# The feed-forward stage of a decoder layer as seven block products in place of eight

## What is computed

```python
D_MODEL = 1024
D_FF = 2816
    x = x + merged @ wo
    h = rmsnorm(x, g_ffn)
    a, u = jnp.split(h @ w_gu, 2, axis=-1)
    return x + (jax.nn.silu(a) * u) @ w_dn
```

## Time and profile before

| what | value |
|---|---|
| time, median of 3 runs | 996.94 us (992.06 to 997.19) |
| time of the profiled execution | 996.81 us |
| its span | 995.0 us |
| busy over the span: PE, DVE, ACT, POOL | 97%, 51%, 34%, 8% |
| the feed-forward stage | about 583 to 981 us of the span |

### The profile page before, as it was taken

The page is one execution under the profiler, slowest core; times in us unless marked ns, Lnnn a source line. Parts: engine busy times, 40 slices in busy tenths (PEclk is TensorE's granted clock), DMA queues, the critical chain, the costliest instruction groups (busy, mean ns, idle before and its releaser), DMA issues.

```text
span 995.0 us, 18231 instructions
## 1 busy us (share of the span) xinstructions
PE 967.9 (97%) x7611; PEld 945.0 (95%) x7611; DVE 507.7 (51%) x933; ACT 335.9 (34%) x559; POOL 77.6 (8%) x107
## 2 busy tenths in 40 slices
PE   6999999999999899999999999999999999999997
PEld 5899999999989889899999999999999999999997
DVE  5735556544887472635355565554445555333232
ACT  7344223444544350422222342222222222222222
POOL 0100013011210200111023000000000000000000
PEclk9899999999999999999999999999999999999999
DMA  7582326432320766122222345222222222222302
GB/s 240 153 262 42 48 77 95 156 108 77 98 65 1 218 192 200 43 86 85 86 86 85 127 147 189 85 88 92 99 96 95 86 85 75 85 75 80 111 1 91
DMA packets 104909, 104.77 MB, mean 105 GB/s; under 512 B 11130, under 2 KB 101752, under 8 KB 104492
## 3 DMA queue, kind: packets, MB, share of 16 engines
q1 hardware_dynamic: 101224, 92.51, 30.3%
q0 software_dynamic: 3552, 11.08, 3.7%
q10 hardware_dynamic: 52, 0.01, 0.0%
HBM read 97.74 MB, written 15.45 MB: 114 GB/s over the span
## 4 chain that ended last, share of the span: by engine, by line
PE 86%; SPq 3%; DVE 3%; ACT 2%; issue 2%; DMA 1%; POOL 1%; ACTq 0%; DVEq 0%; POOLq 0%
PE acc L466 74%; SPq L698 3%; PE acc L1168 1%; PE acc L1081 1%; POOL mt L854 1%; PE acc L1057 1%; PE acc L935 1%; PE acc L924 1%; PE acc L895 1%; PE acc L1041 1%; PE acc L1252 1%; ACT h_hi L1562 1%; DVE w_lo L449 0%; PE acc L1069 0%; DVE mt L1670 0%
## 5 line engine op out<-in xcount | busy, mean ns | idle before, releaser
L466 PE MATMUL acc<-h_hi,w_hi 128*128 128x256 f32 (+1 forms) x1520 | 462.0, 304 | 3.1 <-DVE w_lo L449 2.1
L466 PE MATMUL acc<-h_lo,w_hi 128*128 128x256 f32 (+1 forms) x1520 | 439.2, 289 | 0.0
L466 PE MATMUL acc<-h_hi,w_lo 128*128 128x256 f32 (+1 forms) x1504 | 433.0, 288 | 0.0
L466 PEld LDWEIGHTS acc<-h_hi,w_hi 128*128 128x128 f32 x1520 | 287.6, 189 | 12.0 <-issue 5.1
L466 PEld LDWEIGHTS acc<-h_lo,w_hi 128*128 128x128 f32 x1520 | 288.0, 189 | 4.1 <-issue 2.4
L439 ACT ACTIVATE w_hi<-raw 128x1024 fp32r<-128x1024 f32 (+1 forms) x135 | 140.9, 1043 | 444.9 <-PE acc L466 444.9
L466 PEld LDWEIGHTS acc<-h_hi,w_lo 128*128 128x128 f32 x1504 | 285.0, 189 | 0.0
L449 DVE TENSOR_TENSOR w_lo<-raw,w_hi 128x1024 fp32r<-128x1024 f32 (+1 forms) x134 | 164.0, 1224 | 107.6 <-ACT w_hi L439 102.9
L466 PE MATMUL acc<-s_hi,w_hi 128*128 128x256 f32 (+1 forms) x352 | 101.6, 288 | 0.0
L466 PE MATMUL acc<-s_lo,w_hi 128*128 128x256 f32 (+1 forms) x352 | 101.3, 288 | 0.0
L466 PE MATMUL acc<-s_hi,w_lo 128*128 128x256 f32 (+1 forms) x352 | 100.7, 286 | 0.0
(11 more groups left out here) (348 smaller groups left out, 1122.6 us busy)
## 6 DMA issues: line engine op xcount, KB each, us to landing
raw<-in_w_in SPq DMA_DIRECT2D x25, 1024.0 KB, 5.3
raw<-in_w_gate_up SPq DMA_DIRECT2D x22, 1024.0 KB, 4.9
raw<-in_w_down SPq DMA_DIRECT2D x8, 1024.0 KB, 4.7
rev<-tab POOLq DMA_DIRECT2D x1, 4352.0 KB, 19.4
ring<-in_cache_dsa_kv SPq DMA_DIRECT2D x4, 1024.0 KB, 7.3
raw<-in_w_out SPq DMA_DIRECT2D x4, 1024.0 KB, 5.1
out<-in_cache_dsa_kv SPq DMA_DIRECT2D x2, 2016.0 KB
ring<-in_cache_moba_k SPq DMA_DIRECT2D x48, 64.0 KB, 2.1
```

What stands on the lines that cost most here:

```text
L466: ins = nc.tensor.matmul(acc[:, bank, 0:HALF[half]], a[:, k, :], two(b[:, kx + k, :], half), start=first and k == k0 and c == 0, stop=last ...
```

## The change

Outputs, inputs and tokens of each product are cut in two: a pair of output tiles `m`, a pair of input tiles `k` (even and odd), two halves of 272 tokens. The 2x2 by 2x2 block product is then formed with seven products (a form of Strassen's, with chained sums) for eight. `gate` and `up` are 11 pairs of output tiles each with 4 pairs of input tiles (`depth` 4); `down` is 4 pairs of output tiles, its 11 pairs of input tiles in four chunks of 2, 3, 3 and 3 (`KPS`). That makes 38 pairs, with 7 products each: a stream of 266 products, each of 3 x depth matmuls of 272 columns.

- Four sums of weight blocks for each pair go to GpSimd (`w_sums`), each over depth x 128 columns; one is written in place over `raw`.
- High and low parts of the seven weight operands are made product by product, 128 x (depth x 128), in a ring of six slots, five products ahead (`w_highs` on ACT, `w_lows` on DVE).
- Seven activation operands for each pair of input tiles: DVE forms four sums of 272 columns (`b_sum`), ACT the high parts, DVE the low parts, for `h` during the output projection and for `s` after each `up`.
- Products share partial sums through PSUM: ACT copies a bank into the bank that the next product adds to (`bank_seeds`), or into SBUF (`u2p5`), four copies a pair. DVE takes four results of 272 columns a pair, and scales or adds the first half of the tokens in one further instruction (`second_half`).
- The multiplication of the gate by its sigmoid moves from DVE to GpSimd (`gated_up`). `h_hi`, `h_lo`, `s_hi`, `s_lo` give way to buffers of seven operands.
- The virtual times, banks and semaphores follow; the last norm and the stores stay as they were but for their banks.

The diff, cut to its core:

```diff
+        h7_hi = Map(h_at)("h7_hi", [P, KD // 2, 7, TH], F32R)
+        ga = Map(h_at + 4 * (KD // 2) * 7 * TH)("ga", [P, 2, T])
         m = Map(region)
-        s_hi, s_lo = (m(n, [P, KF, T], F32R) for n in ("s_hi", "s_lo"))
-        sg = m("sg", [P, 2, T])
-        gx = sq
+        s7_hi = m("s7_hi", [P, 3, 7, TH], F32R)
+        h7_lo = m("h7_lo", [P, KD // 2, 7, TH], F32R)
+        wsum = m("wsum", [P, 2, 2, 512])
+        wx_hi, wx_lo = (m(n, [P, 2, 512], F32R) for n in ("wx_hi", "wx_lo"))
+        sv = m("sv", [P, 8, TH])
+        xs2 = m("xs2", [P, 2, TH])
+        s7_lo = m("s7_lo", [P, 3, 7, TH], F32R)
+        u2p5 = m("u2p5", [P, 2, TH])
...
-        for j in range(0, KF, 2):
-            add_load([(0, 0, rows(w_gu, 0, KD, j * P, 256))], KD)
-            add_load([(0, 0, rows(w_gu, 0, KD, D_FF + j * P, 256))], KD)
-        n_gu = len(blocks)
-        DOWN = ((0, 8), (8, 16), (16, 22))
-        for j in range(0, KD, 2):
-            for k0, k1 in DOWN:
-                add_load([(0, 0, rows(w_dn, k0, k1, j * P, 256))], k1 - k0)
...
+        KPS = (2, 3, 3, 3)
+        FIRST = (0, 2, 5, 8)
+        pairs = []
+        for c in range(len(KPS)):
+            for m_ in range(KPS[c]):
+                pairs.append(("gate", c, FIRST[c] + m_))
+                if m_ == 0 and c > 0:
+                    pairs += [("down", c - 1, j) for j in range(KD // 2)]
+                pairs.append(("up", c, FIRST[c] + m_))
+        pairs += [("down", len(KPS) - 1, j) for j in range(KD // 2)]
+        NPAIR = len(pairs)
...
+        stream = []
+        for n in range(NPAIR):
+            if follows(n):
+                if n:
+                    stream += [(n - 1, 4), (n - 1, 3)]
+                stream += [(n, p) for p in (1, 5, 6, 2, 7)]
+            else:
+                stream += [(n, 1), (n - 1, 4), (n - 1, 3)] + [(n, p) for p in (6, 5, 7, 2)]
+        stream += [(NPAIR - 1, 4), (NPAIR - 1, 3)]
+        pos = {np_: i for i, np_ in enumerate(stream)}
+        RING, LEAD = 6, 5
+        B_SLOT = {1: 0, 3: 1, 2: 2, 5: 3, 6: 4, 7: 5, 4: 6}
...
+        def w_source(n, p):
+            if p in (1, 2, 4, 7):
+                return w_part(n, *{1: (0, 0), 2: (0, 1), 4: (1, 1), 7: (1, 0)}[p])
+            return w_sum(n, 0 if p == 5 else 1)
...
+            if n - 3 >= ffn_load:
+                sp.wait_ge(w_lo_done, n_wout + pos[n - 3 - ffn_load, 3] + 1)
...
+                def w_sums():
+                    for n in range(NPAIR):
+                        at = pos[n, 1]
+                        yield tm(at - 5)
+                        pool.wait_ge(mm_done, mm_at[n_merge])
+                        w_ready(pool, n)
+                        if n >= 2:
+                            pool.wait_ge(w_lo_done, n_wout + pos[n - 2, 3] + 1)
+                        done = sem("w_sum")
+                        nc.gpsimd.tensor_tensor(w_sum(n, 0), w_part(n, 1, 0), w_part(n, 1, 1), ALU.add).then_inc(done, 1)
+                        yield tm(at - 4)
+                        pool.wait_ge(done, 4 * n + 1)
+                        nc.gpsimd.tensor_tensor(w_sum(n, 1), w_sum(n, 0), w_part(n, 0, 0), ALU.subtract).then_inc(done, 1)
+                        yield tm(at - 2.5)
+                        nc.gpsimd.tensor_tensor(w_part(n, 1, 0), w_part(n, 0, 0), w_part(n, 1, 0), ALU.subtract).then_inc(done, 1)
+                        yield tm(at - 1)
+                        pool.wait_ge(done, 4 * n + 3)
+                        pool.wait_ge(w_lo_done, n_wout + pos[n, 6] + 1)
+                        nc.gpsimd.tensor_tensor(w_sum(n, 1), w_part(n, 0, 1), w_sum(n, 1), ALU.subtract).then_inc(done, 1)
+                def gated_up():
+                    g = 0
+                    for n in range(NPAIR):
+                        kind, c, j = pairs[n]
+                        if kind == "gate":
+                            yield lag(n, T_GATE)
+                            for m in range(2):
+                                pool.wait_ge(sem("sg_done"), 2 * j + m + 1)
+                                nc.gpsimd.tensor_tensor(ga[:, m, :], ga[:, m, :], sg[:, m, :], ALU.mult).then_inc(sem("t_done"), 1)
+                Side(w_sums(), gated_up()).until(Side.END / 2)
...
+                def claim(n):
+                    for name in ("b", "c"):
+                        nc.tensor.matmul(bank(n, name), h7_hi[:, 0, 0, 0:P], h7_hi[:, 0, 0, :], start=True, stop=True)
+                def product(i):
+                    n, p = stream[i]
+                    kind, c, j = pairs[n]
+                    hi, lo, slot = w_slot(i, False), w_slot(i, True), B_SLOT[p]
+                    b_his, b_los, q0 = (s7_hi, s7_lo, 4 + FIRST[c]) if kind == "down" else (h7_hi, h7_lo, 0)
+                    name = {1: "a", 2: "a", 5: "e", 3: "e", 6: "b", 7: "c", 4: "c"}[p]
+                    pe.wait_ge(w_lo_done, n_wout + i + 1)
+                    if p == 1 and n >= 2:
+                        pe.wait_ge(ffn_ev, evacs[n - 2, 2])
+                    if p == 5 and n >= 2:
+                        pe.wait_ge(ffn_ev, evacs[n - 2, 3])
+                    if p in (6, 7):
+                        pe.wait_ge(seeded, seeds[n, "b" if p == 6 else "c"])
+                    if p == 4:
+                        pe.wait_ge(ffn_ev, evacs[n, 7])
+                    if p == 3:
+                        pe.wait_ge(seeded, seeds[n, "p5"])
+                    for k in range(depth(n)):
+                        if n == 0 or (kind == "down" and j == 0):
+                            pe.wait_ge(b_lo, 2 * KD + b_ready(q0 + k, slot))
+                        for z, (a, b) in enumerate(((hi, b_his), (hi, b_los), (lo, b_his))):
+                            ins = nc.tensor.matmul(bank(n, name), a[:, k, :], b[:, k, slot, :], start=p in (1, 5) and k == 0 and z == 0,
+                                                   stop=k == depth(n) - 1 and z == 2, skip_group_check=True)
+                    ins.then_inc(mm_done, 1)
...
-                        nc.scalar.activation(h_hi[:, k, :], xT[:, k, :], ACT.Copy, scale=vecs[:, 8 + k:9 + k]).then_inc(sem("h2_hi_done"), 1)
+                        if k >= 2 and k % 2 == 0:
+                            act.wait_ge(b_lo, 2 * KD + k // 2)
+                        nc.scalar.activation(s_tile[:, k % 2, :], xT[:, k, :], ACT.Copy, scale=vecs[:, 8 + k:9 + k]).then_inc(sem("hs_done"), 1)
...
+                def b_his(q, slots, hi):
+                    nc.scalar.copy(hi[:, slots, :], sv[:, 1 + slots.start:1 + slots.stop, :]).then_inc(b_hi, 1)
...
+                def w_highs():
+                    for i in range(len(stream)):
+                        n, p = stream[i]
+                        yield tm(i - LEAD) + 0.005 if i >= 4 else n_wout - 0.94 + 0.05 * i
+                        w_ready(act, n)
+                        slot_free(act, i)
+                        if p in (5, 6, 7, 3):
+                            act.wait_ge(sem("w_sum"), 4 * n + {5: 1, 6: 2, 7: 3, 3: 4}[p])
+                        nc.scalar.activation(w_slot(i, False), w_source(n, p), ACT.Copy).then_inc(w_hi_done, 1)
...
+                def bank_seeds():
+                    for i, n, what in copies:
+                        yield tm(i + 1)
+                        act.wait_ge(mm_done, products_done + i + 1)
+                        if what == "b":
+                            src, dst = bank(n, "a"), bank(n, "b")
+                        elif what == "c":
+                            if n >= 2:
+                                act.wait_ge(ffn_ev, evacs[n - 2, 4])
+                            src, dst = bank(n, "b"), bank(n, "c")
+                        elif what == "u2":
+                            if n >= 1:
+                                act.wait_ge(ffn_ev, evacs[n - 1, 3])
+                            src, dst = bank(n, "b"), u2p5[:, 0, :]
+                        else:
+                            if n >= 1:
+                                act.wait_ge(ffn_ev, evacs[n - 1, 7])
+                            src, dst = bank(n, "e"), u2p5[:, 1, :]
+                        nc.scalar.copy(dst, src).then_inc(seeded, 1)
...
+                def b_sum(out, a, b, name):
+                    nc.vector.tensor_tensor(sv[:, out, :], sv[:, a, :], sv[:, b, :], ALU.subtract).then_inc(sem(name), 1)
+                def b_low(slots, hi, lo):
+                    nc.vector.tensor_tensor(lo[:, slots, :], sv[:, 1 + slots.start:1 + slots.stop, :], hi[:, slots, :].bitcast(F32),
+                                            ALU.subtract).then_inc(b_lo, 1)
...
+                        b_sum(4, 0, 1, "b_sum")
+                        b_sum(6, 2, 0, "b_sum")
+                        dve.wait_ge(sem("b_sum"), 4 * q + 1)
+                        b_sum(5, 2, 4, "b_sum")
+                        dve.wait_ge(sem("b_sum"), 4 * q + 3)
+                        b_sum(7, 3, 5, "b_sum")
+                        yield n_merge + 2 * q + 2.7
+                        dve.wait_ge(b_hi, 2 * KD + q + 1)
```

(103 more changed lines are left out.)

285 lines of the change are left out of this document (176 added, 109 removed).

## The result

The changed kernel takes 1072.32 us (median of 4 runs, 1072.08 to 1076.13) against 994.81 us before (4 runs): a ratio of 1.079, 95% interval 1.075 to 1.083. Its profiled execution has a span of 1070.3 us. The side was forecast, the size was not: 77.5 us more, where 21.7 were predicted.

A forecast was written before the change was run, and what follows sets the result against it. PE bounds the old kernel; in the changed stage, POOL additions and DVE two-input instructions taking turns would. 996.8 + 13.2 (stage) + 8.5 (edges) = 1018.5 us; range 975 to 1050, the forecast's own 1002 to 1045.

The forecast's parts named there:

- the exclusion of POOL's additions and DVE's two-input instructions: Feed-forward stage: the two kinds run in turn, so the stage takes 411.1 us against 397.9, +13.2 us.
- three meetings in the trace of before: Overlaps of POOL additions and DVE instructions in the old profile: the later one ends 1.08 or 1.20 us after the earlier.
- The in-turn prices: POOL additions: 1.20 us for 544 columns, 1.13 for 512; DVE behind POOL costs its columns, behind DVE 65 ns more.
- the pace of PE without waits: Feed-forward stage: PE takes 0.1256 us a matmul, for columns that average 272.
- PE stays the bound: Rival for the whole kernel: the gains stand in full, 956 us; chance 0.25 together with a half-way form at 982 us.
- The one of whole instructions in turn: Rival: POOL and DVE each cost full recorded length in turn, gate plus up 29.5 us, time about 1059 us; chance 0.10.
- the step from exclusive work to time: Gate plus up: POOL 11.4 and DVE 13.9 sum to 25.3 us, plus 1.2 for PSUM results, 26.5 us.
- I charge it nothing: ACT in gate plus up: 16 us of work in 21.1, covered by the ring's five products of lead, so no cost.
- the small down pairs and the edges: Down: 5.6 us a pair at depth 2, 8.1 at depth 3; edges of the stage: 8.5 us together.
- The start: End of the output projection: a chain of some 4 us, partly covered by two products, costs 1.5 us (0 to 3).
- The clock: PE where it idles: a granted clock below 1.00 was named as a way to be wrong, without a price.
- The gain that was hoped for: PE in the feed-forward stage: 396 fewer matmuls, worth 49.7 us.

The follow-up runs named there:

- experiments 1 to 4: Changed kernel, GpSimd's weight sums replaced: short memsets 1003.82 us; doubled memsets 1005.51; small memsets plus unused additions 1073.3; short memsets in every second pair 1041.81.
- experiment 7: Changed kernel with 28 further matmuls with unused results ahead of the wait for the first bank copy behind each gate pair, at ten places: 1073.89 us.
- experiments 5, 6: Changed kernel with sigmoids 2.2 products later in ACT's order: 1059.87 us; the same with GpSimd's weight sums replaced by short memsets: 982.92 us.
- Experiment 6: Changed kernel with GpSimd's weight sums replaced by short memsets and the sigmoids 2.2 products later in ACT's order: 982.92 us.

## Why the prediction was wrong

**Right.** That the exclusion of POOL's additions and DVE's two-input instructions decides, not any engine's own load, was read from three meetings in the trace of before; experiments 1 to 4 show it. The in-turn prices held (0.55 us behind a sum for 512 columns, 0.87 for 816), and so did the pace of PE without waits. Of the rivals, "PE stays the bound" falls, and its 956 us does not come with the sums left out either (1003.82, with the sigmoids later 982.92). The one of whole instructions in turn gave a time nearer to the measured (1059), but for a reason that the timelines contradict: with the whole recorded length in turn, as the prediction read the lock on the SBUF — State Buffer page of the Trainium skill, a low part would end 0.69 and 1.01 us behind a sum. The measurement decides.

**Wrong: the step from exclusive work to time.** I summed 25.3 us of exclusive work for gate plus up, added 1.2 for PSUM results and called it 26.5. Where no down pair lies between them, the sigmoids of successive gates start 28.6, 25.3, 28.6, 29.7, 29.2, 27.7 and 27.0 us apart, mean 28.0. The prices themselves held: in these seven stretches POOL or a DVE instruction with two SBUF inputs is at work for 24.8 us on average, POOL or any DVE instruction for 26.2 us. In the other 1.8 us both stand idle, which the sum had no room for. In part of it DVE stands for ACT's high parts, which wait for PE to free a slot of the ring. A sum of two engines' work is a lower bound when both also wait for third parties. The period is 1.5 us over the forecast, eleven times: 16 us.

**Wrong: "I charge it nothing" for ACT.** Its load was right (about 50%), its order was not read. Behind each gate pair the sigmoid stands ahead of a bank copy that PE needs, and in the last down pairs the squares and scalings of the last norm do. The last four down pairs take from 1005.33 to 1053.60 us, 12.1 us each where 8.1 were predicted, 16 us in all. Of these, 8.5 us are waits for ACT's copies, and 7.8 us are matmuls at the lower clock, whose cause stays open (experiment 7). Behind the gates the stall is real but shared: its removal gives 12.4 us beside the sums and 20.9 without them (experiments 5, 6).

**Wrong: the small down pairs and the edges.** One stretch with four pairs of depth 2 and one gate and up takes 57.3 us (664.11 to 721.38): less 28.0, 7.3 us a pair, not 5.6. With depth 3 it is 62.7 us (779.66 to 842.32, and 62.6 in the other one): 8.7 us, not 8.1. Together 11 us. Here it is not idleness: POOL or DVE is at work for 56.4 and 61.8 us of these two stretches. The exclusive work itself was priced too low, 5.0 and 7.1 us a pair where the traces have 7.2 and 8.5; which of its parts is longer was not followed up. Low parts of `s` were late at all four changes to down, where I priced only the last, though that one's 5.5 us is what I had written (5 to 9). The start cost 2.3 + 3.4 + 3.0 us in three waits, not 1.5. These terms, 16 + 16 + 11 + 7 = 50 us, leave some 4 of the 53.8 us between 1018.5 and 1072.3 without a place.

**The clock.** It was named as an unpriced way to be wrong. It fell, and experiment 7 shows that behind the gates it was not what made the kernel slow; for the last four down pairs this is not shown.

**The gain that was hoped for.** The 49.7 us of PE were there. Experiment 6 keeps 12.5 of them with the sums free; with complete work the best was 1029.06 us, 3.5% above the 994.6 us of the kernel before beside it. No version that computes everything beat the kernel before.

## What to carry to other kernels

Taking matmuls away pays only if the vector work that replaces them fits on one engine beside what it does already: work moved from DVE to GpSimd is not parallel when both read SBUF, and one trace row in which both are stretched is enough to find that out. When two engines are priced in turn, treat the sum as a lower bound, and read each engine's fixed order for what stands ahead of the instruction that the bottleneck waits for; the engine's load says nothing about that. A low clock beside waits is to be tested by filling the waits before it is blamed.

## What the runs showed of the hardware beyond expectation

- GpSimd writes do not slow DVE (687 ns for 512 columns, whether a memset overlaps or not), GpSimd additions that read SBUF do (1052 ns on average), even if nobody waits for their results. A low part of 512 columns that starts under an addition ends 0.55 us behind it, in 72 cases out of 72.
- Work with two SBUF inputs cost less on DVE than on GpSimd beside it: moving the weight sums over, with the sigmoids late in both, took the time from 1059.87 to 1040.68 us, and moving the gate's products too, from 1040.68 to 1029.06 us, with DVE over 90% busy already.
- After waits of about 6 us PE came back at the lower clock level and a matmul of 272 columns took 0.56 us; with the waits filled the mean granted clock rose from 0.91 to 0.96 and the time did not change (1072.3 and 1073.9 us).
